# A sparse-expert block on one core: expert blocks of 32 rows in four column groups instead of 64 rows in two

## The chip, the cores and the metric

The program runs on one NeuronCore of one Trainium2 chip. The metric is the device time of one execution in microseconds (us); of the kernel before, three executions are given. Engines are named as the profile names them: PE (TensorE, with PEld for its weight loads), DVE (VectorE), ACT (ScalarE), POOL (GpSimd) and SP (SyncE).

## The reference

528 rows (16 learned ones and 512 tokens) of 1024 numbers go through one layer: a combined attention part, and then a layer of 32 experts of which each token takes its best four. Only the second part is touched:

```python
logits = xf @ w_router + b_router
top_val, top_idx = lax.top_k(logits, 4)
gates = softmax(top_val)
# for each token and each of its four experts e:
act = clamped_swiglu(x @ w1[e] + b1[e])      # w1[e]: 1024 x 2048
out[token] += gate * (act @ w2[e] + b2[e])   # w2[e]: 1024 x 1024
```

`clamped_swiglu` splits the 2048 columns into a gate and a linear half, clips both at 7, and gives gate * sigmoid(1.702 * gate) * (linear + 1). Everything is float32. An expert's weights are 12.58 MB, those of all 32 are 403 MB.

## The kernel before, in words

Attention, router and tables take the first 510 us or so of the span and are left as they are. The layer of experts takes the rest. It works in **blocks**: a block is up to SLOTS = 64 of the 512 * 4 = 2048 (token, expert) pairs, all of one expert. An expert with n pairs has ceil(n / 64) blocks, at least one. A token's 1024 numbers are stored as two rows of 512 (`xfd`), and the result as well (`accd`), so a block is 128 partitions: 64 slots times 2 half rows.

For block g the engines do, each in its own program order:

- DVE (`slot_list`, `slot_rows`) finds which tokens are in the block, with one small product on PE (`slot_product`, L1278), and writes their row numbers to `gidx`.
- POOL (`gather`, L445 and L446) fetches the rows by an indirect DMA into the one buffer `xg`.
- PE (`turn_x`, L1272) transposes `xg`, and ACT (`xT_copy`, L637) copies it to `xT`.
- PE (`up`, L1299 and L1305) makes the hidden layer: 8 contraction tiles k, two parts (gate, linear), two halves n of 512 columns. The stationary operand is 64 slots wide, and the two halves n go to partitions 0 to 63 and 64 to 127 of a bank, that is to two column groups of the array. L1305 adds the bias.
- DVE (`hidden`, L988 to L993) with ACT (L642) makes the activation `gat[b]`; PE (L1334) transposes it, and ACT (L655) copies it to `actT`.
- PE (`down`, L1326, bias L1341) makes the output in bank 4.
- DVE (L1018) scales it by the gate into the one buffer `yb` and keeps the row numbers (L1020).
- POOL (L466 and L467) adds the rows into `accd` by an indirect DMA that reads, adds and writes. Two such adds must not be in flight together, since they can touch one row; so POOL waits for the end of each (L470, and L471 marks it).

PE's loop over g is: `up(g+1)`, transposes of `gat(g)`, `turn_x(g+2)`, `slot_product(g+3)`, `down(g)`. SP fetches the weights in the order in which experts are worked on, into two sets of buffers (even and odd places): `w1` of the expert two places on is issued when the last `up` of this one is done (L383), and `w2` when the last `down` is done (L388). The order alternates experts with more than 64 pairs and others, as long as there are any.

The rows of each expert follow from the inputs. Reckoned from the reference's own router, the counts of the 32 experts are 83, 55, 79, 78, 107, 53, 17, 35, 43, 52, 104, 68, 116, 36, 99, 145, 59, 16, 8, 24, 38, 47, 44, 71, 90, 127, 51, 43, 57, 87, 42 and 74. In blocks of 64 that is 47 blocks, which is what the trace has; in blocks of 32 it is 81.

Of the kernel before, what the change touches and what calls it, by code (L numbers as in the profile page):

```python
# [30 lines left out]
P = 128  # L31
# [9 lines left out]
SLOTS = 64  # L41
# [12 lines left out]
C_ID, C_SLOT, C_EXP, C_D, C_B = 0, 128, 256, 320, 321  # L54
NCA = 322

T_TRI, T_ONE, T_IE, T_IG, T_THR = 0, 128, 256, 288, 288 + NG
NCT = T_THR + 8
# [12 lines left out]
def shape_constants():  # L71
# [4 lines left out]
    a[:, C_SLOT:C_SLOT + P] = c % SLOTS  # L76
    a[:, C_EXP:C_EXP + SLOTS] = np.where(p < 3 * NE, p % NE, -1)
# [5 lines left out]
    ct[:, T_THR:T_THR + 7] = SLOTS * np.arange(1, 8)  # L83
    ct[:, T_THR + 7] = 1e9
    half = (np.arange(P) >= SLOTS) * 1.0
# [29 lines left out]
def build(nc, I, out):  # L115
    ctx = ExitStack()
    with ctx:
# [80 lines left out]
        xg = work[:, 0:512]  # L198
        xT = work[:, 512:1024].rearrange("p (j n) -> p j n", j=4)
        gat = [work[:, 1024:1536], work[:, 1536:2048]]  # L200
        actT = work[:, 2048:2560].rearrange("p (j n) -> p j n", j=4)
# [15 lines left out]
        nbt = work[0:NE, o:o + 12]  # L217
        i8u = work[:, o + 13:o + 21].bitcast(U32)
        o += 21
# [18 lines left out]
        yb = sb("yb", [P, 512])[:, :]  # L238
# [12 lines left out]
        sidc = sb("sidc", [P, 1], I32)  # L251
# [38 lines left out]
        gather_turn, rows_turn, idx_kept = sem("gather_turn"), sem("rows_turn"), sem("idx_kept")  # L290
# [114 lines left out]
        def _(pool):  # L405
# [4 lines left out]
            zero = Steps(pool, zeros_ready)  # L410
            zero(nc.gpsimd.memset(qz[HD:P, :, 0, :], 0.0))
# [28 lines left out]
            def gather(n):  # L440

                if not (isinstance(n, int) and n == 0):
                    pool.wait_ge(gather_turn, n)
                pool.wait_ge(list_ready, n + 1)
                nc.gpsimd.tensor_tensor(sm[:, 36:37], ones1, ones1, ALU.mult).then_inc(gather_turn, 1)  # L445
                pool.indirect_dma_start(out=xg, out_offset=None, in_=xfd, in_offset=bass.IndirectOffsetOnAxis(  # L446
                    ap=gidx[:, 0:1], axis=0)).then_inc(xg_in, 16)
# [6 lines left out]
            nc.gpsimd.tensor_tensor(sm[:, 37:38], ones1, ones1, ALU.mult).then_inc(rows_turn, 1)  # L454
            nc.gpsimd.tensor_tensor(sm[:, 21:22], ones1, ones1, ALU.mult).then_inc(added, 1)
# [4 lines left out]
            with pool.Fori(0, MAXBLK) as g:  # L460
                with pool.If(g < nb):
                    pool.wait_ge(xT_done, g + 3)
                    gather(g + 3)
                    pool.wait_ge(rows_turn, g + 1)
                    pool.wait_ge(y_ready, 2 * g + 2)
                    nc.gpsimd.tensor_tensor(sm[:, 37:38], ones1, ones1, ALU.mult).then_inc(rows_turn, 1)  # L466
# [4 lines left out]
                    nc.gpsimd.tensor_tensor(sm[:, 21:22], ones1, ones1, ALU.mult).then_inc(added, 1)  # L471
                pool.nop()
# [5 lines left out]
        def _(act):  # L478
# [40 lines left out]
            for u, (g, f) in enumerate(units):  # L519
# [3 lines left out]
                if nq == 0:  # L523
                    act.wait_ge(zeros_ready, 2)
# [11 lines left out]
            def stick_log(hh):  # L536
                act.wait_ge(z_done, hh + 1)
                if hh == 0:
                    act.wait_ge(zeros_ready, 8)
# [51 lines left out]
            def diff_squares(i):  # L591
# [3 lines left out]
                act.activation(yb[:, 0:P], oall[:, i, :], ACT.Square,  # L595
# [39 lines left out]
            def xT_copy(n):  # L635
                act.wait_ge(xT_done, n + 1)
                act.activation(xT, PS[:, 7, :].rearrange("p (j n) -> p j n", j=4), ACT.Copy)\  # L637
                    .then_inc(xT_ready, 1)

            def sigmoid(n, b):  # L640
                act.wait_ge(gat_ready, n + 1)
                act.activation(PS[:, 2 * b, :], gat[b], ACT.Sigmoid, scale=HID_ALPHA).then_inc(sig_ready, 1)  # L642
# [28 lines left out]
        def _(dve):  # L671
# [237 lines left out]
            step(nc.vector.tensor_scalar(place[:, 0:1], nbt[:, 9:10], 1.0, None, ALU.is_gt))  # L909
# [3 lines left out]
            step(nc.vector.tensor_copy(nb2[:, 0:1], nbt[:, 9:10]))  # L913
# [18 lines left out]
            step(nc.vector.tensor_tensor(place[:, 8:9], place[:, 6:7], nbt[:, 9:10], ALU.subtract))  # L932
# [16 lines left out]
            def selector(n, b):  # L949

                nc.vector.tensor_scalar(selb[:, b, :], ca[:, C_EXP:C_EXP + SLOTS], egf[:, bass.ds(n, 1)], None,
                                        ALU.is_equal).then_inc(sel_ready, 1)

            def slot_list(n):
# [5 lines left out]
                for t in range(TT):  # L960
                    nc.vector.tensor_scalar(slots[:, t, :], ca[:, C_SLOT:C_SLOT + P], b64[:, bass.ds(n, 1)],  # L961
# [431 lines left out]
```

## Time and profile before

| what | value |
|---|---|
| three executions | 1656.5, 1657.3, 1658.1 us, median 1657.3 |
| the profiled execution: its span, first to last instruction | 1652.7 us |
| the same execution with what lies around the span | no time of its own is given; the median is 4.6 us above the span |
| PE busy | 1503.6 us, 91% of the span |
| POOL, ACT, DVE busy | 195.2, 266.2, 444.0 us |
| HBM read and written | 442.9 and 20.5 MB |
| TensorE clock, mean granted | 0.962 |
| products of `up` (L1299) and `down` (L1326), busy | 661.4 and 333.1 us |

A float32 product appears as two MATMUL records, so a block has 64 records of L1299 and 32 of L1326. Busy times of PE are unions: records of two column groups run at the same time, and the mean duration of one (597 ns) is longer than the time that each costs.

### The profile page before, as it was taken

To read this page: it belongs to the slowest core of one execution; us is meant where nothing else is said; L and a number is where in the kernel's file an instruction comes from. 1 tells how busy PE (TensorE), PEld (TensorE's weight loads), DVE (VectorE), ACT (ScalarE), POOL (GpSimd) and SP (SyncE) were. 2 spreads that over 40 slices of the span, in tenths; PEclk is the share of its full clock that TensorE was granted. 3 is DMA by queue.
4 is the path that set the end of the run, shared out by engine and by line. 5 is a ranking of instruction groups with operands and counts; after the bars stand their busy time and mean duration, and the time that the engine had idled before them with its cause. 6 is when DMAs were issued, how large, how long until landed. Compare 5 with 4: busy or idle time off the path is not lost.

```text
span 1652.7 us, 20407 instructions
## 1 busy us (share of the span) xinstructions
PE 1503.6 (91%) x6812; PEld 647.6 (39%) x6813; DVE 444.0 (27%) x1254; ACT 266.2 (16%) x444; POOL 195.2 (12%) x280
## 2 busy tenths in 40 slices
PE   5999988977965999999999999999999999999782
PEld 3746533355442343333334333333334334334231
DVE  3010123276253212222122221222212222122122
ACT  3001035343111101111011110111101111011012
POOL 5300000000000111111111111111111111111011
PEclk9999999987976999999999999999999999999997
DMA  9310020021645599999999999995999999999994
GB/s 322 98 38 0 0 102 0 0 106 64 254 156 226 224 349 374 413 374 406 374 374 413 374 406 373 374 370 223 388 375 405 380 394 388 368 406 383 406 403 140
DMA packets 95470, 463.71 MB, mean 281 GB/s; under 512 B 7316, under 2 KB 7572, under 8 KB 62676
## 3 DMA queue, kind: packets, MB, share of 16 engines
q1 hardware_dynamic: 84084, 436.90, 66.3%
q0 software_dynamic: 10976, 26.03, 6.3%
q10 hardware_dynamic: 384, 0.44, 0.1%
q8 instruction: 16, 0.26, 0.1%
q14 instruction: 10, 0.08, 0.0%
HBM read 442.86 MB, written 20.48 MB: 280 GB/s over the span
## 4 chain that ended last, share of the span: by engine, by line
PE 83%; DMA 5%; DVE 4%; issue 3%; ACT 2%; SPq 2%; POOL 0%; DVEq 0%; POOLq 0%; ACTq 0%
PE PS L1299 37%; PE PS L1326 18%; DMA sb_arena<-in_w 4%; PE PS L1067 3%; PE PS L1195 3%; PE PS L1073 3%; PE PS L1070 2%; PE PS L1071 2%; PE PS L1334 2%; PE PS L1272 1%; PE PS L1305 1%; PE PS L1091 1%; PE PS L1125 1%; PE PS L1104 1%; SPq L383 1%
## 5 line engine op out<-in xcount | busy, mean ns | idle before, releaser
L1299 PE MATMUL PS<-sb_arena,sb_work 128*64 128x512 f32 x3008 | 661.4, 597 | 17.8 <-DMA sb_arena<-in_w 16.1
L1299 PEld LDWEIGHTS PS<-sb_arena,sb_work 128*64 128x64 f32 x3008 | 230.7, 138 | 439.3 <-issue 414.7
L1326 PE MATMUL PS<-sb_arena,sb_work 128*64 128x512 f32 x1504 | 333.1, 595 | 13.0 <-issue 13.0
L988 DVE TENSOR_SCALAR sb_work<-PS 128x512 f32<-128x512 f32 x47 | 32.5, 692 | 638.3 <-PE PS L1305 638.3
L1326 PEld LDWEIGHTS PS<-sb_arena,sb_work 128*64 128x64 f32 x1504 | 112.9, 137 | 205.8 <-issue 205.4
L655 ACT ACTIVATE sb_work<-PS 128x512 f32<-128x512 f32 x47 | 28.1, 598 | 944.2 <-PE PS L1334 944.2
L467 POOL DMA_INDIRECT accd<-sb_yb,sb_sidc x47 | 75.4, 1605 | 7.2 <-issue 3.8
L1018 DVE TENSOR_SCALAR sb_yb<-PS,sb_gates 128x512 f32<-128x512 f32 x47 | 35.3, 751 | 131.5 <-PE PS L1326 131.5
L961 DVE TENSOR_SCALAR sb_slots<-sb_ca,sb_b,sb_rk 128x128 bf16<-128x128 f32 x204 | 56.9, 373 | 36.8 <-issue 36.8
L653 ACT ACT_TABLE_LOAD x47 | 60.3, 1283 | 0.8
L1195 PE MATMUL PS<-sb_arena 128*128 128x512 f32 x128 | 57.0, 604 | 1.5 <-DVE sb_arena L846 1.5
L445 POOL TENSOR_TENSOR sb_sm<-sb_sm 128x1 f32<-128x1 f32 x50 | 9.7, 193 | 410.8 <-DVE sb_gidx L979 410.3
L1067 PE MATMUL PS<-sb_arena 128*128 128x512 f32 x128 | 56.9, 606 | 0.6 <-DVE sb_work L713 0.6
L1073 PE MATMUL PS<-sb_arena 128*128 128x512 f32 x128 | 55.3, 592 | 0.0
L446 POOL DMA_INDIRECT sb_work<-xfd,sb_gidx x50 | 50.5, 1010 | 8.3 <-issue 2.2
L471 POOL TENSOR_TENSOR sb_sm<-sb_sm 128x1 f32<-128x1 f32 x47 | 8.9, 190 | 344.7 <-DMA accd<-sb_yb,sb_sidc 344.7
L1179 PE MATMUL PS<-sb_arena 128*128 128x128 f32 x112 | 22.8, 363 | 18.7 <-ACT sb_arena L587 17.4
L1070 PE MATMUL PS<-sb_arena 128*128 128x264 f32 x128 | 38.9, 386 | 0.0
L1071 PE MATMUL PS<-sb_arena 128*128 128x264 f32 x128 | 38.9, 386 | 0.0
L1067 PEld LDWEIGHTS PS<-sb_arena 128*128 128x128 f32 x128 | 24.8, 195 | 32.5 <-issue 31.3
L991 DVE TENSOR_TENSOR sb_work<-sb_work,PS 128x512 f32<-128x512 f32 x47 | 32.3, 688 | 18.9 <-ACT PS L642 18.9
L1195 PEld LDWEIGHTS PS<-sb_arena 128*128 128x128 f32 x128 | 24.6, 195 | 31.3 <-issue 29.5
(250 smaller groups left out, 1154.1 us busy)
## 6 DMA issues: line engine op xcount, KB each, us to landing
sb_arena<-in_w SPq DMA_DIRECT2D x192, 2048.0 KB, 20.6
sb_arena<-in_w_in SPq DMA_DIRECT2D x6, 2048.0 KB, 21.8
sb_arena<-in_x SPq DMA_DIRECT2D x8, 512.0 KB, 7.0
sb_arena<-in_w_out SPq DMA_DIRECT2D x2, 2048.0 KB, 10.7
accd<-sb_arena SPq DMA_DIRECT2D x4, 512.0 KB, 6.6
xfd<-sb_arena SPq DMA_DIRECT2D x4, 512.0 KB, 4.7
sb_arena<-accd SPq DMA_DIRECT2D x4, 512.0 KB, 6.6
out<-sb_arena SPq DMA_DIRECT2D x4, 512.0 KB, 2.8
```

The source lines that it names most:

```text
L446: pool.indirect_dma_start(out=xg, out_offset=None, in_=xfd, in_offset=bass.IndirectOffsetOnAxis(ap=gidx[:, 0:1], axis=0)).then_inc(xg_in, 16)
L467: pool.indirect_dma_start(out=acc, out_offset=bass.IndirectOffsetOnAxis(ap=sidc[:, 0:1], axis=0), in_=yb, in_offset=None, compute_op=ALU.a ...
L653: act.preload_act_table(ACT.Sigmoid)
L961: nc.vector.tensor_scalar(slots[:, t, :], ca[:, C_SLOT:C_SLOT + P], b64[:, bass.ds(n, 1)], rk[:, t, bass.ds(e, 1)], ALU.add, ALU.is_equal)\
L1018: nc.vector.tensor_scalar(yb, PS[:, 4, :], gates[:, bass.ds(g, 1)], None, ALU.mult)\
L1067: last = mm(PS[:, b, :], w[:, k, f * P:(f + 1) * P], nT[:, k, META:NKEY], **io)
L1070: mm(PS[:, b, 0:n], w[:, k, f * P:(f + 1) * P], nT[:, k, 0:n], **io)
L1071: last = mm(PS[:, b + 1, 0:n], w[:, k, f * P:(f + 1) * P], nT[:, k, n:NKEY], **io)
L1073: last = mm(PS[:, b, :], nT[:, k, META + f * P:META + (f + 1) * P], w[:, k, :], **io)
L1195: last = mm(PS[:, u % 4, :], mixT[:, k, t * P:(t + 1) * P], wo[:, n, k, :], start=k == 0, stop=k == KT - 1)
L1299: mm(PS[half(n), 2 * b + part, :], xT[:, k % 4, half(k // 4)], w[:, k, c:c + 512], start=k == 0, stop=False)
L1326: last = mm(PS[half(n), 4, :], actT[:, k % 4, half(k // 4)], w[:, k, n * 512:(n + 1) * 512], start=False, stop=k == KT - 1)
```

## The change

SLOTS becomes 32. A block is now 32 slots times 2 half rows, that is R = 64 partitions.

- `up` writes four column groups of 32 partitions into one bank: gate columns in groups 0 and 1, linear columns in 2 and 3. The number of products in a block is the same, each with a stationary operand of 32 columns instead of 64.
- `down` is split over the contraction too: the halves s of the contraction and the halves n of the columns go to four column groups, and the two halves s are added by DVE (`outputs`, one instruction more).
- The transposes stay 128 by 128 (rows 64 to 127 are filler); the copies of ACT take half the columns.
- Gathers and row adds move 64 rows each instead of 128.
- `yb` and `sidc` are doubled, and POOL's loop is turned round: it issues the row add of block g+1 in the turn of g, after it has seen the end of that of g.
- Tables for 81 instead of 47 blocks are a little longer.

```diff
-SLOTS = 64
+SLOTS = 32
...
-        gat = [work[:, 1024:1536], work[:, 1536:2048]]
+        gatp = [work[:, 1024:1536], work[:, 1536:2048]]
+        gat = [x[0:R, :] for x in gatp]
...
+            def scatter(n, b):
+
+                pool.wait_ge(added, n + 2)
+                pool.wait_ge(y_ready, 3 * n + 3)
+                nc.gpsimd.tensor_tensor(sm[:, 21:22], ones1, ones1, ALU.mult).then_inc(scatter_turn, 1)
+                pool.indirect_dma_start(out=acc, out_offset=bass.IndirectOffsetOnAxis(
+                    ap=sidc[0:R, b:b + 1], axis=0), in_=yb[b], in_offset=None,
+                    compute_op=ALU.add).then_inc(y_out, 16)
...
-            with pool.Fori(0, MAXBLK) as g:
-                with pool.If(g < nb):
-                    pool.wait_ge(xT_done, g + 3)
-                    gather(g + 3)
-                    pool.wait_ge(rows_turn, g + 1)
-                    pool.wait_ge(y_ready, 2 * g + 2)
-                    nc.gpsimd.tensor_tensor(sm[:, 37:38], ones1, ones1, ALU.mult).then_inc(rows_turn, 1)
-                    pool.indirect_dma_start(out=acc, out_offset=bass.IndirectOffsetOnAxis(ap=sidc[:, 0:1], axis=0),
-                                            in_=yb, in_offset=None, compute_op=ALU.add).then_inc(y_out, 16)
-                    pool.wait_ge(added, g + 1)
-                    pool.wait_ge(y_out, g * 16 + 16)
-                    nc.gpsimd.tensor_tensor(sm[:, 21:22], ones1, ones1, ALU.mult).then_inc(added, 1)
-                pool.nop()
+            scatter(0, 0)
+            with pool.Fori(0, (MAXBLK + 1) // 2) as i:
+                for b in range(2):
+                    g = 2 * i + b
+                    with pool.If(g < nb):
+                        pool.wait_ge(xT_done, g + 3)
+                        gather(g + 3)
+                        pool.wait_ge(scatter_turn, g + 1)
+                        pool.wait_ge(y_out, g * 16 + 16)
+                        nc.gpsimd.tensor_tensor(sm[:, 37:38], ones1, ones1, ALU.mult).then_inc(added, 1)
+                        with pool.If(g + 1 < nb):
+                            scatter(g + 1, 1 - b)
+                        pool.nop()
+                    pool.nop()
...
-                        dve.wait_ge(y_done, g + 1)
-                        dve.wait_ge(added, g + 1)
-                        nc.vector.tensor_scalar(yb, PS[:, 4, :], gates[:, bass.ds(g, 1)], None, ALU.mult)\
-                            .then_inc(y_ready, 1)
-                        nc.vector.tensor_copy(sidc[:, :], sidx[:, bass.ds(g, 1)]).then_inc(y_ready, 1)
+            def outputs(n, b):
+
+                gate = gates[0:R, bass.ds(n, 1)]
+                dve.wait_ge(y_done, n + 1)
+                dve.wait_ge(added, n + 1)
+                nc.vector.tensor_scalar(yb[b], PS[0:R, 4, :], gate, None, ALU.mult).then_inc(y_ready, 1)
+                nc.vector.tensor_copy(sidc[:, b:b + 1], sidx[:, bass.ds(n, 1)]).then_inc(y_ready, 1)
+                dve.wait_ge(y_ready, 3 * n + 2)
+                nc.vector.scalar_tensor_tensor(yb[b], PS[R:P, 4, :], gate, yb[b], ALU.mult, ALU.add)\
+                    .then_inc(y_ready, 1)
...
-                    for part in range(2):
-                        for n in range(2):
-                            c = part * D + n * 512
-                            mm(PS[half(n), 2 * b + part, :], xT[:, k % 4, half(k // 4)], w[:, k, c:c + 512],
-                               start=k == 0, stop=False)
+                    for c in range(4):
+                        mm(PS[group(c), b, :], xT[:, k % 4, group(k // 4)], w[:, k, c * 512:(c + 1) * 512],
+                           start=k == 0, stop=False)
...
-                for k in range(KT):
-                    if k % 4 == 0:
-                        pe.wait_ge(w2_full[par][k // 4], (at_place // 2) * 16 + 16)
-                    for n in range(2):
-                        last = mm(PS[half(n), 4, :], actT[:, k % 4, half(k // 4)], w[:, k, n * 512:(n + 1) * 512],
-                                  start=False, stop=k == KT - 1)
+                for j in range(4):
+                    for s in range(2):
+                        k = 4 * s + j
+                        if j == 0:
+                            pe.wait_ge(w2_full[par][s], (at_place // 2) * 16 + 16)
+                        for n in range(2):
+                            last = mm(PS[group(2 * s + n), 4, :], actT[:, j, group(s)],
+                                      w[:, k, n * 512:(n + 1) * 512], start=s == 1 and j == 0, stop=j == 3)
```

POOL's loop shows the new order. Before, one turn of the loop, for block g (`xfd` is read by the gather, `accd` is written by the row add; names in brackets are semaphores):

```order
L444 REGISTER_ALU [waits gather_turn,xT_done]
L445 TENSOR_TENSOR sb_sm<-sb_sm 128x1 [waits list_ready]
L446 DMA sb_work<-xfd,sb_gidx 128x512
L464 REGISTER_ALU
L465 ISA [waits rows_turn]
L466 TENSOR_TENSOR sb_sm<-sb_sm 128x1 [waits y_ready]
L467 DMA accd<-sb_yb,sb_sidc 1152x512
L470 ISA [waits added]
L471 TENSOR_TENSOR sb_sm<-sb_sm 128x1 [waits y_out]
```

With the change, one turn of the loop, on POOL as well (line numbers are those of the changed kernel here and below):

```order
L451 REGISTER_ALU [waits gather_turn,xT_done]
L452 TENSOR_TENSOR sb_sm<-sb_sm 128x1 [waits list_ready]
L453 DMA sb_work<-xfd,sb_gidx 64x512
L483 REGISTER_ALU
L484 ISA [waits scatter_turn]
L485 TENSOR_TENSOR sb_sm<-sb_sm 128x1 [waits y_out]
L486 COMPARE_AND_BRANCH
L466 ISA [waits added]
L467 TENSOR_TENSOR sb_sm<-sb_sm 128x1 [waits y_ready]
L468 DMA accd<-sb_work,sb_sidc 1152x512
```

In the turn of g the row add is that of g before, behind the gather of g+3; now it is that of g+1, so that the gather of g+3 stands behind the row add of g.

The other place is what DVE does with a block's output. Before:

```order
L1018 ISA [waits added,y_done]
L1018 TENSOR_SCALAR sb_yb<-PS,sb_gates 128x512
L1020 REGISTER_ALU
L1020 COPY sb_sidc<-sb_sidx 128x1
L951 ISA
L951 TENSOR_SCALAR sb_selb<-sb_ca,sb_egf 128x64
```

With the change, on DVE:

```order
L1019 ISA [waits added,y_done]
L1019 TENSOR_SCALAR sb_work<-PS,sb_gates 64x512
L1020 REGISTER_ALU
L1020 COPY sb_sidc<-sb_sidx 128x1
L1021 ISA
L1022 SCALAR_TENSOR_TENSOR sb_work<-PS,sb_gates,sb_work 64x512 [waits y_ready]
L968 ISA
L968 TENSOR_SCALAR sb_selb<-sb_ca,sb_egf 128x32
```

One instruction of 512 columns is added (L1022), which waits for the one ahead of it, and POOL's row add waits for it.

## Rows read from the trace of the kernel before

**Rows 1.** The page: busy time by engine, and the costliest group of instructions.

```profile
PE 1503.6 (91%) x6812; PEld 647.6 (39%) x6813; DVE 444.0 (27%) x1254; ACT 266.2 (16%) x444; POOL 195.2 (12%) x280
...
L1299 PE MATMUL PS<-sb_arena,sb_work 128*64 128x512 f32 x3008 | 661.4, 597 | 17.8 <-DMA sb_arena<-in_w 16.1
```

**Rows 2.** Busy time by stage, 1160 to 1500 us; columns in its first line.

```profile
core 0: us, PE busy (x) PEld busy (x) DVE busy (x) ACT busy (x) POOL busy (x), PEclk, DMA share, GB/s
...
1160.00:1500.00 340.00, 335.68 (x1691) 130.31 (x1688) 85.76 (x252) 43.28 (x60) 46.06 (x73) 1.00 0.99 391
```

**Rows 3.** Timeline of PE: start us, us, engine, line, operation, count, [idle before].

```profile
550.03 0.61 PE L1305 MATMUL PS<-sb_ball,sb_selb 128*64 128x512 bf16 x4
550.57 0.66 PE L1334 MATMUL PS<-sb_ca,sb_work 128*128 128x128 f32 x4
551.07 0.60 PE L1272 MATMUL PS<-sb_ca,sb_work 128*128 128x128 f32 x4
...
552.29 7.09 PE L1326 MATMUL PS<-sb_arena,sb_work 128*64 128x512 f32 x32 [0.21 <-issue]
559.20 13.91 PE L1299 MATMUL PS<-sb_arena,sb_work 128*64 128x512 f32 x64
...
573.47 0.66 PE L1334 MATMUL PS<-sb_ca,sb_work 128*128 128x128 f32 x4
```

**Rows 4.** Timeline of DVE after the down products of one block.

```profile
559.53 0.75 DVE L1018 TENSOR_SCALAR sb_yb<-PS,sb_gates 128x512 f32<-128x512 f32 x1 [2.67 <-PE PS L1326]
560.20 0.14 DVE L1020 COPY sb_sidc<-sb_sidx 128x1 int32 x1
```

**Rows 5.** Timeline of POOL: gathers (L446), row adds (L467), ends of adds (L471).

```profile
560.43 0.19 POOL L466 TENSOR_TENSOR sb_sm<-sb_sm 128x1 f32<-128x1 f32 x1 [4.29 <-DVE sb_sidc L1020]
560.77 1.63 POOL L467 DMA_INDIRECT accd<-sb_yb,sb_sidc  x1 [0.15 <-issue]
...
583.66 1.60 POOL L467 DMA_INDIRECT accd<-sb_yb,sb_sidc  x1
592.31 0.19 POOL L471 TENSOR_TENSOR sb_sm<-sb_sm 128x1 f32<-128x1 f32 x1 [7.05 <-DMA accd<-sb_yb,sb_sidc]
...
692.88 1.01 POOL L446 DMA_INDIRECT sb_work<-xfd,sb_gidx  x1
...
1111.69 1.60 POOL L467 DMA_INDIRECT accd<-sb_yb,sb_sidc  x1 [0.15 <-issue]
1116.46 0.20 POOL L471 TENSOR_TENSOR sb_sm<-sb_sm 128x1 f32<-128x1 f32 x1 [3.17 <-DMA accd<-sb_yb,sb_sidc]
...
1621.38 0.19 POOL L445 TENSOR_TENSOR sb_sm<-sb_sm 128x1 f32<-128x1 f32 x1 [0.47 <-issue]
1622.13 1.00 POOL L446 DMA_INDIRECT sb_work<-xfd,sb_gidx  x1 [0.57 <-issue]
```

**Rows 6.** Timeline, the first gather and the transposes that waited for it.

```profile
508.49 1.05 POOL L446 DMA_INDIRECT sb_work<-xfd,sb_gidx  x1 [0.15 <-issue]
...
511.98 1.12 PE L1272 MATMUL PS<-sb_ca,sb_work 128*128 128x128 f32 x4 [4.99 <-DMA sb_work<-xfd,sb_gidx]
```

**Rows 7.** DMA queues, 692.8 to 697.1 us: packets, MB, share of 16 engines.

```profile
q1 hardware_dynamic: 435, 1.81, 105.2%
```

**Rows 8.** DMA queues, 697.1 to 699.7 us.

```profile
q1 hardware_dynamic: 101, 0.80, 75.5%
q0 software_dynamic: 80, 0.26, 25.6%
```

**Rows 9.** Timeline of PE near the end, where it waits for weights.

```profile
1553.27 5.18 PE L1299 MATMUL PS<-sb_arena,sb_work 128*64 128x512 f32 x16 [3.07 <-DMA sb_arena<-in_w]
1558.95 3.65 PE L1299 MATMUL PS<-sb_arena,sb_work 128*64 128x512 f32 x16 [0.50 <-DMA sb_arena<-in_w]
...
1585.23 3.65 PE L1299 MATMUL PS<-sb_arena,sb_work 128*64 128x512 f32 x16 [2.77 <-DMA sb_arena<-in_w]
```

**Rows 10.** Busy time of the stretch behind the wait of 3.07 us.

```profile
1553.00:1556.40 3.40, 3.13 (x8) 1.00 (x10) 0.00 (x0) 0.00 (x0) 0.20 (x1) 0.50 1.01 420
```

More of the change, by code:

```diff
@@ L75, in shape_constants @@
     a[:, C_ID:C_ID + P] = p == c
-    a[:, C_SLOT:C_SLOT + P] = c % SLOTS
-    a[:, C_EXP:C_EXP + SLOTS] = np.where(p < 3 * NE, p % NE, -1)
+    a[:, C_SLOT:C_SLOT + SLOTS] = np.arange(SLOTS)
+    a[:, C_EXP:C_EXP + 1] = np.where(p < 3 * NE, p % NE, -1)
     ct = np.zeros((P, NCT), np.float32)
@@ L82, in shape_constants @@
     ct[:, T_IG:T_IG + NG] = np.arange(NG)
-    ct[:, T_THR:T_THR + 7] = SLOTS * np.arange(1, 8)
-    ct[:, T_THR + 7] = 1e9
-    half = (np.arange(P) >= SLOTS) * 1.0
+    ct[:, T_THR:T_THR + THR - 1] = SLOTS * np.arange(1, THR)
+    ct[:, T_THR + THR - 1] = 1e9
+    half = (np.arange(P) // SLOTS) % 2 * 1.0
     spare = 2 * T + np.arange(P)
@@ L197, in build @@
         work = sb("work", [P, 5 * 512])
[L198 to L201 removed]
+        R = 2 * SLOTS
+        xgp = work[:, 0:512]
+        xg = xgp[0:R, :]
+        xT = work[:, 512:768].rearrange("p (j n) -> p j n", j=4)
+        actT = work[:, 768:1024].rearrange("p (j n) -> p j n", j=4)
+        gatp = [work[:, 1024:1536], work[:, 1536:2048]]
+        gat = [x[0:R, :] for x in gatp]
         ct = work[:, 0:NCT]
@@ L216, in build @@
         o += NG // 2
-        nbt = work[0:NE, o:o + 12]
-        i8u = work[:, o + 13:o + 21].bitcast(U32)
-        o += 21
+        nbt = work[0:NE, o:o + 20]
+        nblk = nbt[:, 1 + THR:2 + THR]
+        i8u = work[:, o + 20:o + 28].bitcast(U32)
+        o += 28
         hot = work[0:NE, o:o + NREL]
@@ L237, in build @@
         g6 = sb("g6", [P, TT, NE, 6], BF16)
-        yb = sb("yb", [P, 512])[:, :]
+        yrow = sb("yb", [P, 512])[:, :]
+        yb = [yrow[0:R, :], work[0:R, 2048:2560]]
         rk = sb("rk", [P, TT, NE])
@@ L410, in _ @@
             zero = Steps(pool, zeros_ready)
+            zero(nc.gpsimd.memset(work[R:P, 1024:2048], 0.0))
             zero(nc.gpsimd.memset(qz[HD:P, :, 0, :], 0.0))
@@ L594, in diff_squares @@
                     act.wait_ge(osq_done, i)
-                act.activation(yb[:, 0:P], oall[:, i, :], ACT.Square,
+                act.activation(yrow[:, 0:P], oall[:, i, :], ACT.Square,
                                accum_out=ssd[:, i:i + 1]).then_inc(osq_done, 1)
@@ L636, in xT_copy @@
                 act.wait_ge(xT_done, n + 1)
-                act.activation(xT, PS[:, 7, :].rearrange("p (j n) -> p j n", j=4), ACT.Copy)\
+                act.activation(xT, PS[:, 7, :].rearrange("p (j n) -> p j n", j=4)[:, :, 0:R], ACT.Copy)\
                     .then_inc(xT_ready, 1)
@@ L1285, in expert, with group @@
                                      min_val=0, max_val=NE - 1)
-            def half(n):
+            def group(n):
                 return slice(n * SLOTS, (n + 1) * SLOTS)
@@ L1295, in up @@
                         pe.wait_ge(w1_full[par][k // 2], (at_place // 2) * 16 + 16)
-                    for part in range(2):
-                        for n in range(2):
-                            c = part * D + n * 512
-                            mm(PS[half(n), 2 * b + part, :], xT[:, k % 4, half(k // 4)], w[:, k, c:c + 512],
-                               start=k == 0, stop=False)
-                pe.wait_ge(sel_ready, g + 1)
-                for part in range(2):
-                    for n in range(2):
-                        c = part * D + n * 512
-                        last = mm(PS[half(n), 2 * b + part, :], selb[:, b, :], ball[:, c:c + 512],
-                                  start=False, stop=True)
+                    for c in range(4):
+                        mm(PS[group(c), b, :], xT[:, k % 4, group(k // 4)], w[:, k, c * 512:(c + 1) * 512],
+                           start=k == 0, stop=False)
+                pe.wait_ge(sel_ready, g + 1)
+                for c in range(4):
+                    last = mm(PS[group(c), b, :], selb[:, b, :], ball[:, c * 512:(c + 1) * 512],
+                              start=False, stop=True)
                 last.then_inc(up_done, 1)
@@ L1340, in finish_block @@
                 for n in range(2):
-                    mm(PS[half(n), 4, :], selb[:, b, :], ball[:, 2 * D + n * 512:2 * D + (n + 1) * 512],
+                    mm(PS[group(n), 4, :], selb[:, b, :], ball[:, 2 * D + n * 512:2 * D + (n + 1) * 512],
                        start=True, stop=False)
```

58 lines of the change are left out of this document (30 added, 28 removed).

## The prediction

> **What bounds the kernel now.** First I read the page's busy times: PE is busy for 91% of the span, and its largest group, the products of `up`, waits only 17.8 us in all, 16.1 of them for weights [rows 1]. So PE sets the pace. Second, the stages: in 340 us of the expert layer PE is busy for 335.7 at full clock, but the DMA engines are at 0.99 too, moving 391 GB/s [rows 2]. Two limits lie side by side, and taking work from PE alone can't gain much. Third, PE's timeline: from one block's transposes (550.57) to the next one's (573.47) are 22.90 us, of which `up` takes 13.91 and `down` 6.91 (552.29 to 559.20) [rows 3]. The 47 blocks and the waits make 47 * 22.90 + 17.8 = 1094 us.
>
> **PE's own work per block.** The 64 records of `up` cost 13.91 / 64 = 0.217 us each because two column groups run at once [rows 3]. With four at once a record costs half: `up` falls by 6.9 us, `down` by 3.5, the bias products of L1305 (0.54 to the next row) by 0.2. The transposes and the small products stay. A block then costs PE 22.90 - 10.6 = 12.3 us, say 12.4. No row shows four groups at once. The bounds are this and no overlap beyond two, which leaves 22.9; I take the full overlap, because two groups now show no loss at all (a record of 512 columns lasts 0.6 us and a pair costs 0.43), and it is the nearer row. By PE alone the layer would be 81 * 12.4 = 1004 us.
>
> **What DMA allows.** 30 experts' weights (377.5 MB; the first two are fetched mostly ahead) and 81 gathers and adds of 0.13 MB each way are 399 MB. At 391 GB/s [rows 2] that is 1020 us, so even at best no more than some 75 us are to be had.
>
> **The new loop through POOL.** This is the term that decides. The gather of block g+3 stands on POOL behind the row add of g, which waits for DVE's outputs of g, which wait for `down(g)`. The gather is needed by `turn_x(g+3)`, which PE reaches after only one `up`. Before, that gather was issued ahead of the add of g and had all of `down(g)` and a 13.9 us `up` as cover; now its cover is an `up` of 7 us. One turn, from the start of one `turn_x` to that of the next:
>
> - `turn_x` to the first product of `down`: 552.29 - 551.07 = 1.2 us [rows 3];
> - `down`: half of 7.09, with its tail 3.6 [rows 3];
> - end of `down` (559.38) to POOL's L466 (560.43): 1.05 us [rows 3 to 5], and the added DVE instruction, taken as long as its neighbour's 0.75 [rows 4] with 0.1 for its wait: 1.9;
> - L466 to the issue of the add: 0.34 [rows 5];
> - the issue: 1.6 us for 128 rows [rows 5]; for 64 between 0.8 (all of it per row) and 1.6 (none); I take 1.3;
> - from the add's end to the gather's start on a POOL that is itself late: 0.47 + 0.75 = 1.2 (the two rows from 1621.38) [rows 5];
> - the gather's flight.
>
> Without the flight that is 9.8 us. The flight is 3.5 us when nothing else is in the queues (508.49 to 511.98, reader included) [rows 6]. While weights are streaming it is longer: a gather issued at 692.88 [rows 5] had moved nothing by 697.1, when only the weight queue had packets [rows 7], and its 80 packets fell in the next 2.6 us [rows 8], so it took between 4.2 and 6.8 us. The row adds agree: 8.65 us to the row behind them with weights in flight, 4.77 without [rows 5]. With half the rows I take 2.9 and 6.1. The turn is then 12.7 us in a quiet queue and 15.9 behind weights, against 12.4 of PE's work: PE waits up to 3.5 us in a block. Bounds: 9.3 + 5.2 = 14.5 to 10.1 + 6.8 = 16.9 behind weights, 12.4 to 13.6 without.
>
> The Trainium skill (DMA: Bandwidth & Descriptors, Queues, rings and completion order) says that each DMA engine goes round its queues packet by packet, by which a gather would hardly feel the weights; rows 7 and 8 contradict that for this kernel, and the measurement decides. What follows if it held for smaller gathers is the first rival.
>
> **The clock.** Near the end PE waits 3.07 us, and the next 16 records take 5.18 us instead of 3.65 [rows 9], since the clock was granted at 0.50 for that stretch, that is 1.2 instead of 2.4 GHz [rows 10]; after a wait of 2.77 us they take 3.65 [rows 9]. A wait of 3.5 us per block lies above both, so this may cost 0 to 1.5 us in each such block. I take 0.5: a slow stretch that falls on `up` is covered by the same wait.
>
> **Other terms.** Row adds stay in order; the add of g+1 waits for the end of that of g, some 7 us after the start of a turn plus 8.7 [rows 5], which is before the next is due at 7 + 16, so double buffering neither costs nor gives. It only hides a wait of POOL for which PE was not waiting. ACT's copies and DVE's steps of a block (under 9 us of busy time) are covered by a turn of 12 or more; longer tables and one more memset at the start cost a microsecond at most, beside loads. Waits for weights shrink, since the stage becomes slower than DMA: the 17.8 us go.
>
> **The sum.** Weights stream for 377.5 MB / 391 GB/s = 965 us, three quarters of a stage of 1250, so 60 blocks of 81 turn in 15.9 + 0.5 = 16.4 us and 21 in 12.7: 984 + 267 = 1251 us, against 1094. That is +157: the profiled span of 1652.7 becomes 1810, and the median of 1657.3, which is 4.6 above it, **1814**. With the low bounds 60 * 14.5 + 21 * 12.4 = 1130, +36; with the high ones and the whole clock term 60 * 18.4 + 21 * 13.6 = 1390, +296. Most of this case lies in 1715 to 1900.
>
> **Rival 1, the gather is quick enough; faster or level.** If a gather of 64 rows waits for about one weight packet per packet of its own, its flight stays near 3 us and the turn near 12.6. Then weights set the pace where experts are small: 5 of the 15 later pairs of experts have only 4 blocks, 50 us of PE against 25.2 MB / 391 GB/s = 64 us of DMA. 81 * 12.6 + 5 * 14 = 1091, and with 12.4 a block 1074: 1637 to 1655, **1645**. For it: fewer packets. Against it: the delay in rows 7 and 8 lies ahead of the first packet, and fewer rows don't shorten that. The point at which it decides is a flight of about 3 us behind weights. The skill's round-robin rule above speaks for this rival. Chance 0.21.
>
> **Rival 2, four groups overlap only in part.** If a record costs 0.135 us and not 0.108, PE's block is 15 us and the turn 0.9 longer, so 60 * 17.3 + 21 * 15 = 1353, +259: **1916**. The Trainium skill (TensorE: Matmul & The Clock Gate, Measured speedup vs the span model) has 2.38 times from three column tiles, which is such a loss of a fifth; no row here shows one for two. Chance 0.08.
>
> **Rival 3, the change doesn't do what it says:** the groups run two at a time as now, and 81 blocks cost 22.9 each: 1855, +761, **2418**. Chance 0.04.
>
> **How the numbers follow.** My forecast has 0.67. A difference of less than 0.2% (3.3 us) can't be told from no change here. Rival 1 gives 0.16 of faster and 0.04 of same, the rest of it is just slower; my case and rivals 2 and 3 are slower, 0.80 in all. The range holds my case but for its upper end and rival 1 but for its lowest part: 1640 to 1900. My case's own is 1715 to 1900.
>
> **What the profile after would show.** Right: 81 blocks; L1323 at about 6.9 us a block; most of PE's idle time in front of L1298, released by the gather's DMA, some 3 us each; a PE clock below 1.00 in many slices; DMA below 0.85 in the layer. Wrong: PE's waits in front of L1323 and L1350, released by weights, with DMA at 0.99 (rival 1); `up` at 8.6 us (rival 2) or 13.9 (rival 3).

## The result, and the profile after

The changed kernel takes 2009.59 us (median of 4 runs, 2008.37 to 2016.81) beside 1656.88 us for the kernel before (4 runs, 1653.69 to 1658.1): a ratio of 1.2146, 95% interval 1.2117 to 1.2175. It is slower, as forecast, but by 353 us and not by 157, and lies outside the range. The profiled execution has a span of 2007.3 us, 354.6 more than before.

The page of the changed kernel, busy time and the granted clock by slice, then the groups that answer to [rows 1], and the gather:

```profile
PE 1608.3 (80%) x10688; PEld 630.4 (31%) x10689; DVE 709.9 (35%) x1913; ACT 342.4 (17%) x580; POOL 288.8 (14%) x450
...
PEclk9999899897788887989888888898888888888886
...
L1323 PE MATMUL PS<-sb_arena,sb_work 128*32 128x512 f32 x5184 | 573.9, 594 | 2.2 <-ACT sb_work L654 2.2
...
L1298 PE MATMUL PS<-sb_ca,sb_work 128*128 128x128 f32 x332 | 60.4, 310 | 218.2 <-DMA sb_work<-xfd,sb_gidx 218.2
...
L453 POOL DMA_INDIRECT sb_work<-xfd,sb_gidx x84 | 79.6, 948 | 13.8 <-issue 13.8
```

5184 records of L1323 are 81 blocks of 64. `up` no longer waits for weights at all; nearly all idle time of PE that another engine or a transfer causes (213.7 of 215.9 us) has moved in front of L1298, the transposes of the gathered rows. The granted clock stands at 7 or 8 tenths in nearly every slice of the layer.

PE's waits of the changed kernel, 520 to 1990 us (line, what it waited for, us in total, times, longest; "issue" is idle time for which the profile shows no releaser):

```profile
PE PS L1298 <- DMA sb_work<-xfd,sb_gidx: 213.7, 60, 6.4
PE PS L1365 <- issue: 47.9, 81, 0.6
PE PS L1304 <- issue: 15.4, 49, 0.4
```

Busy time by stage of the changed kernel, to lay beside [rows 2]: us, busy time and count of PE, PEld, DVE, ACT, POOL, then clock, DMA share, GB/s. PE and DMA, both full before, are both partly idle now.

```profile
600.00:1000.00 400.00, 324.36 (x2568) 108.69 (x2564) 147.02 (x400) 57.71 (x88) 69.02 (x114) 0.88 0.76 284
...
1500.00:1900.00 400.00, 318.97 (x2464) 104.65 (x2466) 142.49 (x388) 55.22 (x84) 64.47 (x108) 0.86 0.80 304
```

One turn of the loop behind weights, in three timelines of the changed kernel (start us, us, engine, line, operation, what it writes and reads, count, [idle before and its releaser]). PE, the place of [rows 3]:

```profile
860.61 0.66 PE L1298 MATMUL PS<-sb_ca,sb_work 128*128 128x128 f32 x4 [3.13 <-DMA sb_work<-xfd,sb_gidx]
861.57 0.59 PE L1304 MATMUL PS<-sb_g,sb_slots 128*128 x4 [0.31 <-issue]
862.74 0.61 PE L1365 MATMUL PS<-sb_ball,sb_selb 128*32 128x512 bf16 x2 [0.58 <-issue]
863.42 5.92 PE L1350 MATMUL PS<-sb_arena,sb_work 128*32 128x512 f32 x32
869.14 7.06 PE L1323 MATMUL PS<-sb_arena,sb_work 128*32 128x512 f32 x64
876.01 0.41 PE L1327 MATMUL PS<-sb_ball,sb_selb 128*32 128x512 bf16 x4
...
880.47 0.66 PE L1298 MATMUL PS<-sb_ca,sb_work 128*128 128x128 f32 x4 [3.46 <-DMA sb_work<-xfd,sb_gidx]
```

DVE, the place of [rows 4]:

```profile
869.52 0.74 DVE L1019 TENSOR_SCALAR sb_yb<-PS,sb_gates 64x512 f32<-64x512 f32 x1 [4.18 <-PE PS L1350]
...
870.36 0.75 DVE L1022 SCALAR_TENSOR_TENSOR sb_yb<-PS,sb_gates,sb_yb 64x512 f32<-64x512 f32 x1
```

POOL, the place of [rows 5]:

```profile
871.19 0.20 POOL L467 TENSOR_TENSOR sb_sm<-sb_sm 128x1 f32<-128x1 f32 x1 [11.85 <-DVE sb_yb L1022]
871.53 1.44 POOL L468 DMA_INDIRECT accd<-sb_yb,sb_sidc  x1
872.51 0.70 POOL L452 TENSOR_TENSOR sb_sm<-sb_sm 128x1 f32<-128x1 f32 x1
873.36 0.95 POOL L453 DMA_INDIRECT sb_work<-xfd,sb_gidx  x1 [0.16 <-issue]
```

Read the three together and the ring of the prediction is there, link by link: the transposes at 860.61, `down` from 863.42 to 869.34, DVE to 871.11, POOL's add at 871.53, the gather at 873.36, the next transposes at 880.47 after 3.46 us of idle PE. Of this turn of 19.86 us, 7.11 are the gather. And `up` is what was hoped of four groups: 64 records in 7.06 us against 13.91 before [rows 3].

Why `down` takes 5.92 us here is in the stages of the changed kernel (same columns as above): behind the wait the clock is granted at 0.50, 1.2 instead of 2.4 GHz, and the low stretch covers `down`, not `up`.

```profile
847.60:861.20 13.60, 10.47 (x98) 3.29 (x88) 4.45 (x8) 0.98 (x2) 3.00 (x5) 1.00 0.76 268
861.20:868.00 6.80, 5.84 (x31) 2.08 (x34) 2.22 (x10) 1.67 (x2) 0.00 (x0) 0.50 1.03 423
```

That holds for the whole trace. Of 79 turns (all but the first), 57 begin behind a wait of over 1 us, and `down` takes 4.70 to 6.36 us in every one of them; of the other 22 it takes 3.64 us in 21.

From the same 79 turns I took five pieces, start of the transposes to start of the next. 58 turns end in a wait of over 1 us (the loaded turns; beside them the forecast for turns behind weights), 21 don't (the quiet turns; beside them the one for quiet queues):

| piece of a turn, us | forecast, behind weights | measured, 58 turns | forecast, quiet | measured, 21 turns |
|---|---|---|---|---|
| `turn_x` to first product of `down` | 1.2 | 2.56 | 1.2 | 2.42 |
| `down` | 3.6 | 5.31 | 3.6 | 4.78 |
| end of `down` to L467 | 1.9 | 1.88 | 1.9 | 1.89 |
| L467 to start of the gather | 2.84 | 2.18 | 2.84 | 2.17 |
| start of the gather to the next `turn_x` | 6.1 | 7.16 | 2.9 | 3.48 |
| clock, as a term of its own | 0.5 | in the above | 0 | in the above |
| turn | 16.4 | 19.09 | 12.7 | 14.74 |

The mean of all turns is 17.93 us; 81 of them are 1452 us, against the 1094 of the layer before: +358, within 4 us of the difference of the spans. So the lost time is all in these turns.

The quiet turns need a second look. PE's rows where one of them ends (the next `turn_x` is L1298 at 825.23):

```profile
824.74 0.66 PE L1358 MATMUL PS<-sb_ca,sb_work 128*128 128x128 f32 x4
825.23 0.60 PE L1298 MATMUL PS<-sb_ca,sb_work 128*128 128x128 f32 x4
```

L1298 follows L1358 with no idle time, as in 20 of the 21 quiet turns. So what closes a quiet turn is PE's own work, and the 3.48 us of its last piece are not a gather's flight.

### The profile page after: what moved, and what is told of

Same layout as the page of the kernel before. It is cut to its first block, busy times and chain, and to the rows that moved or that the text cites. A ratio compares the mean times of both kernels' runs of the same rounds, so it can differ in the third digit from the quotient of the medians.

```text
span 2007.3 us, 31695 instructions
## 1 busy us (share of the span) xinstructions
PE 1608.3 (80%) x10688; PEld 630.4 (31%) x10689; DVE 709.9 (35%) x1913; ACT 342.4 (17%) x580; POOL 288.8 (14%) x450
## 4 chain that ended last, share of the span: by engine, by line
issue 59%; PE 22%; POOL 8%; DVE 4%; DMA 3%; ACT 2%; POOLq 1%; SPq 0%; DVEq 0%; ACTq 0%
POOL sb_work L453 4%; PE PS L1093 3%; PE PS L1221 3%; PE PS L1099 3%; POOL sb_sm L452 3%; DMA sb_work<-xfd,sb_gidx 2%; PE PS L1350 2%; PE PS L1096 1%; PE PS L1097 1%; POOL accd L468 1%; PE PS L1117 1%; PE PS L1151 1%; PE PS L1205 1%; PE PS L1323 1%; POOL sb_sm L485 1%
## 5 line engine op out<-in xcount | busy, mean ns | idle before, releaser
L1323 PE MATMUL PS<-sb_arena,sb_work 128*32 128x512 f32 x5184 | 573.9, 594 | 2.2 <-ACT sb_work L654 2.2
L1350 PE MATMUL PS<-sb_arena,sb_work 128*32 128x512 f32 x2592 | 418.2, 804 | 2.4 <-issue 1.0
L1323 PEld LDWEIGHTS PS<-sb_arena,sb_work 128*32 128x32 f32 x5184 | 168.4, 110 | 393.0 <-issue 392.7
L1298 PE MATMUL PS<-sb_ca,sb_work 128*128 128x128 f32 x332 | 60.4, 310 | 218.2 <-DMA sb_work<-xfd,sb_gidx 218.2
L1007 DVE TENSOR_SCALAR PS<-PS 64x512 f32<-64x512 f32 x81 | 56.8, 701 | 423.5 <-PE PS L1327 423.5
L672 ACT ACTIVATE sb_work<-PS 128x256 f32<-128x256 f32 x81 | 31.1, 384 | 1015.0 <-PE PS L1358 1015.0
L1350 PEld LDWEIGHTS PS<-sb_arena,sb_work 128*32 128x32 f32 x2592 | 103.0, 142 | 272.3 <-issue 271.5
L467 POOL TENSOR_TENSOR sb_sm<-sb_sm 128x1 f32<-128x1 f32 x81 | 15.7, 194 | 882.1 <-DVE sb_yb L1022 452.5
L1298 PEld LDWEIGHTS PS<-sb_ca,sb_work 128*128 128x128 f32 x332 | 39.9, 153 | 233.3 <-DMA sb_work<-xfd,sb_gidx 232.5
L1365 PE MATMUL PS<-sb_ball,sb_selb 128*32 128x512 bf16 x162 | 44.5, 543 | 47.9 <-issue 47.9
L1010 DVE TENSOR_TENSOR sb_work<-sb_work,PS 64x512 f32<-64x512 f32 x81 | 55.0, 679 | 53.5 <-ACT PS L659 53.5
L1304 PE MATMUL PS<-sb_g,sb_slots 128*128 x336 | 47.6, 180 | 24.2 <-issue 15.4
L654 ACT ACTIVATE sb_work<-PS 128x256 f32<-128x256 f32 x83 | 31.3, 377 | 195.9 <-PE PS L1298 195.9
L452 POOL TENSOR_TENSOR sb_sm<-sb_sm 128x1 f32<-128x1 f32 x84 | 57.5, 684 | 23.9 <-DVE sb_gidx L998 23.9
L485 POOL TENSOR_TENSOR sb_sm<-sb_sm 128x1 f32<-128x1 f32 x81 | 15.7, 194 | 299.4 <-DMA accd<-sb_yb,sb_sidc 152.1
```

The costliest lines, as they stand in the source:

```text
L1298: last = nc.tensor.transpose(PS[:, 7, j * P:(j + 1) * P], xgp[:, j * P:(j + 1) * P], ident)
L1323: mm(PS[group(c), b, :], xT[:, k % 4, group(k // 4)], w[:, k, c * 512:(c + 1) * 512], start=k == 0, stop=False)
L1350: last = mm(PS[group(2 * s + n), 4, :], actT[:, j, group(s)], w[:, k, n * 512:(n + 1) * 512], start=s == 1 and j == 0, stop=j == 3)
```

## The experiments

The theory at this point: the add ahead of the gather puts the gather's flight into PE's path; the waits it causes bring the low clock, which lengthens `down`, which stands in the same ring. The rivals: PE's smaller blocks or the double-buffered adds cost the time, and the low clock is only a sign of waits; or the order on POOL alone is at fault, whatever the size of a block. A run with one measurement carries no interval; two runs of one kernel differ here by up to 0.8% (1634.41 to 1647.45 for the first below), so nothing under some 13 us is read from it. Experiments 1, 3, 4 and 6 ran on one chip (the kernel before: 1656.92 us), 2, 5 and 7 on another (1652.25).

### 1. The gather ahead of the add again

The one edit that undoes the order on POOL and keeps the rest:

```diff
+            pool.wait_ge(xT_done, 3)
+            gather(3)
             scatter(0, 0)
...
-                    with pool.If(g < nb):
-                        pool.wait_ge(xT_done, g + 3)
-                        gather(g + 3)
+                    with pool.If(g + 1 < nb):
+                        pool.wait_ge(xT_done, g + 4)
+                        gather(g + 4)
...
-                        with pool.If(g + 1 < nb):
-                            scatter(g + 1, 1 - b)
-                        pool.nop()
+                        scatter(g + 1, 1 - b)
```

> Theory (the gather of block g+3 waits on POOL behind the row add of g, and PE waits for it and then runs at the low clock): with the gather issued first, PE's 214 us of waits in front of L1298 go, the granted clock is 1.00 again, and a turn costs 12.4 to 13 us; 81 turns with some 70 us of waits for weights are 1075 to 1120 us against about 1435 now, so 1650 to 1695 us. Rival (81 blocks simply have too many fixed steps, wherever the gather stands): within 2% of 2009 us.

Measured: 1642.09 us (6 runs, 1634.41 to 1647.45), ratio to the kernel before 0.9918, interval 0.9887 to 0.9948. It is 367 us faster than the changed kernel and 0.8% faster than the kernel before; that lies 8 us below the range expected, whose 70 us of waits for weights were too many. Its PE waits, 520 to 1990 us:

```profile
PE PS L1323 <- DMA sb_arena<-in_w: 52.1, 20, 6.4
PE PS L1365 <- issue: 8.8, 20, 0.7
...
PE PS L1298 <- DMA sb_work<-xfd,sb_gidx: 2.0, 1, 2.0
```

Its POOL timeline in one turn, the transposes that the gather is for, and its stage from 600 to 1000 us:

```profile
834.91 1.44 POOL L468 DMA_INDIRECT accd<-sb_yb,sb_sidc  x1
...
843.46 0.95 POOL L453 DMA_INDIRECT sb_work<-xfd,sb_gidx  x1
```

```profile
851.93 0.60 PE L1298 MATMUL PS<-sb_ca,sb_work 128*128 128x128 f32 x4
```

```profile
600.00:1000.00 400.00, 386.62 (x3582) 141.21 (x3578) 202.24 (x562) 79.51 (x124) 95.84 (x157) 0.99 1.01 388
```

The gather starts as soon as its indices are there and has 8.5 us until the transposes at 851.93 need it. The median turn is 12.35 us, the 12.4 worked out for PE alone, the clock is back, and what PE waits for is weights at 388 GB/s. The order on POOL carries the whole loss.

### 2. The adds waited for in the same turn

Is it the double buffering of the adds? This kernel keeps both buffers and the gather first, but waits for each add before the next turn:

```diff
-            scatter(0, 0)
...
                         gather(g + 3)
+                        scatter(g, b)
                         pool.wait_ge(scatter_turn, g + 1)
...
-                        with pool.If(g + 1 < nb):
-                            scatter(g + 1, 1 - b)
-                        pool.nop()
```

> The kernel as changed with POOL's order of before: gather of g+3, row add of g, wait for that add, all in one turn (both buffers for the output rows stay). Theory (the place of the gather is all that matters, the overlapped adds give nothing): POOL is free again 1.9 + 1.8 + 7.3 = 11 us after the end of down, and the next gather can't start before its list, 12.6 us after it (843.12 against the down that ends at 831 in the gather-first run), so the same time as gather first, 1642 us within 8. Rival (the double buffer is what makes gather-first quick): the add's wait shows in the turns, 1 us or more in each, 1720 us or more.

Measured: 1645.95 us (4 runs, 1640.85 to 1651.0), ratio 0.9948, interval 0.9928 to 0.9968; the median turn is 12.37 us. Its waits, all engines, 520 to 1620 us:

```profile
POOL sb_sm L485 <- DMA accd<-sb_work,sb_sidc: 221.2, 40, 6.4
POOL sb_sm L485 <- DMA accd<-sb_yb,sb_sidc: 214.8, 40, 6.3
```

POOL stands 436 us in waits for adds, and PE waits for none of them. The intervals of this kernel and of experiment 1 overlap, so the overlapped adds are worth nothing that these runs can tell. This settles a point which the diff hides: the order on POOL came with the double buffering, and the time is lost by that order, not gained by the buffers.

### 3. The same order in the kernel before

Blocks of 64, two groups, one buffer, as before; only POOL's loop is in the changed order (the add of g+1 at the end of turn g, ahead of the next gather).

```diff
+            pool.wait_ge(rows_turn, 1)
+            scatter(0)
...
-                    pool.wait_ge(rows_turn, g + 1)
-                    pool.wait_ge(y_ready, 2 * g + 2)
...
+                    with pool.If(g + 1 < nb):
+                        scatter(g + 1)
```

> The kernel before (blocks of 64) with the changed kernel's order on POOL: the gather of g+3 behind the row add of g. Theory (the order is harmful only because the cover is now one short up): the loop is 1.2 + 7.1 + 1.05 + 0.34 + 1.6 + 0.4 + 7.0 = 18.7 us, less than a block's 22.9, so no change, 1657 us within 5. Rival (the order of POOL costs by itself, whatever the block's size): at least 3 us more in each of 47 blocks, 1800 us.

Measured: 1664.0 us in one run, beside 1656.92 (9 runs). Its PE waits, 520 to 1990 us:

```profile
PE PS L1306 <- DMA sb_arena<-in_w: 13.6, 7, 3.2
...
PE PS L1279 <- DMA sb_work<-xfd,sb_gidx: 6.9, 1, 6.9
```

One wait for a gather, the first, and the median turn is 22.90 us in both kernels. The order costs nothing that can be told where `up` lasts 13.9 us: the gather, 9.5 us in flight here, is still covered. By the sum of the expectation with 9.5 for its 7.0 the ring is 21.2 us, so it was covered with 1.7 us to spare, not 4.2. So neither the order alone nor the small block alone loses the time (that of experiment 1 has small blocks and is fast); it takes both. The 7.1 us above the kernel before, 2 more than expected at most, are within what one run can't tell.

### 4. The changed kernel with thin weights

To take the weights' traffic away and leave everything else: of each expert but the first two, only 128 of the 2048 columns of w1 and 64 of the 1024 of w2 are fetched; the products run on what lies there. The fetch of the other weights is what this kernel leaves out.

```diff
-                        sp.dma_start(w1t(par)[:, 2 * c:2 * c + 2, :],
-                                     I["w1"][bass.ds(e, 1), 2 * c * P:2 * (c + 1) * P, :]
+                        sp.dma_start(w1t(par)[:, 2 * c:2 * c + 2, 0:128],
+                                     I["w1"][bass.ds(e, 1), 2 * c * P:2 * (c + 1) * P, 0:128]
```

> The kernel as changed, but from the third expert on only one in sixteen columns of its weights is fetched, so that DMA queues are nearly empty (the outputs are then wrong). Theory: every gather lands in 2.5 to 3.4 us, every turn is a quiet one of about 13.3 us, PE waits under 1 us a block and the clock stays up: 81 * 13.3 = 1077 us against 1435, about 1650 us. Rival (the gathers' flight does not depend on the weights): 2009 us within 2%.

Measured: 1647.04 us. Of its PE waits, 520 to 1990 us:

```profile
PE PS L1365 <- issue: 48.7, 81, 0.6
PE PS L1298 <- DMA sb_work<-xfd,sb_gidx: 7.6, 5, 6.5
```

The clock is 1.00 and the mean turn 13.40 us (nine in ten lie between 13.1 and 13.9): 2.21 to `down`, 3.66, 1.94, 2.17, and 3.42 from the gather on. PE waits for a gather in 5 turns only, though the ring's flight of 2.9 us is there in each: this turn is PE's own work. The flight is what changed, as the issues of the trace show, 520 to 1600 us (issues, median us from issue to landing). The changed kernel:

```profile
sb_work<-xfd,sb_gidx POOLq DMA_INDIRECT x61, 7.0
accd<-sb_yb,sb_sidc POOLq DMA_INDIRECT x30, 7.3
```

With thin weights:

```profile
sb_work<-xfd,sb_gidx POOLq DMA_INDIRECT x80, 2.9
accd<-sb_yb,sb_sidc POOLq DMA_INDIRECT x40, 3.7
```

Gather ahead of the add, full weights (experiment 1):

```profile
sb_work<-xfd,sb_gidx POOLq DMA_INDIRECT x81, 6.3
```

Blocks of 64, gather behind an add of 128 rows (experiment 3):

```profile
sb_work<-xfd,sb_gidx POOLq DMA_INDIRECT x46, 9.5
```

Four flights of the gather, three with 64 rows and the last with 128: 2.9 us with hardly any weights in the queues, 6.3 behind weights with no add ahead, 7.0 right behind an add of 64 rows, 9.5 right behind one of 128. The weights' traffic costs a gather of 64 rows some 4 us (7.0 against 2.9, both right behind an add), and the add ahead of it in the same software queue a further 0.7. With 128 rows the gather behind an add takes at least 2.7 us more than the one without, which took 4.2 to 6.8 [rows 7, 8].

### 5. Gather first and thin weights together

Both edits of experiments 1 and 4; it leaves out the same part of the weights.

> Gather first, and from the third expert on one in sixteen columns of the weights is fetched (wrong outputs). Theory (gather first is bound by the weights, not by PE): turns of 12.35 us throughout, 81 * 12.35 = 1000 against about 1075 to 1100, so 1545 to 1565 us. Rival (PE or the small steps bind gather first as well): 1640 us.

Measured: 1550.19 us; the median turn is 12.15 us at a clock of 1.00. Of its PE waits, 520 to 1990 us:

```profile
PE PS L1298 <- DMA sb_work<-xfd,sb_gidx: 2.0, 1, 2.0
PE PS L1365 <- issue: 1.2, 2, 0.6
```

The kernel of experiment 1 is therefore bound by weights: they cost it some 90 us (one run, and on another chip), 52.1 in PE's waits for them, an estimated 26 in the low clock behind such waits (51 us of the layer at 0.50, none here) and 16 in the turns, 0.2 us longer each (12.35 and 12.15). That is the prediction's first paragraph: taking work from PE can't gain much with DMA at 0.99. And L1365 has its gap of 0.6 us in 81 turns of experiment 4 and in 2 of this one, and the turn is 13.40 us there and 12.15 here. The two kernels differ in POOL's order alone.

### 6. Idle products in the wait

Does the low clock cost time in the ring? Here PE does 14 products whose result nobody reads just ahead of the transposes, some 3.2 us more work in each block:

```diff
                 last.then_inc(actT_done, 1)
+                for _ in range(14):
+                    mm(PS[R:P, 3, :], ball[:, 0:R], ball[:, 0:512], start=True, stop=True)
                 turn_x(g + 2)
```

> The kernel as changed, with 14 idle products of 512 columns (3.0 us at full clock) put into the place where PE waits for the gather; they touch no result. If the low clock behind the wait is what lengthens the turns from about 16 to 19.5 us, the clock stays near 1.00, the turns behind weights fall to about 16.4 us and the quiet ones rise from 13.3 to 16.3: 81 * 16.4 = 1330 instead of 1435, about 1900 us, faster by added work. If the clock costs nothing on this path, the long turns stay at 19.5 and only the quiet ones grow: 2060 us or more.

Measured: 1961.41 us, 48 us less than the changed kernel with 260 us more of PE's work:

```profile
L1361 PE MATMUL PS<-sb_ball 128*64 128x512 bf16 x1134 | 259.9, 381 | 0.0
```

Its stages from 600 to 1900 us are at a clock of 0.97, 0.99 and 0.97, and PE's timeline shows what a turn behind weights is with the clock kept:

```profile
837.24 0.66 PE L1298 MATMUL PS<-sb_ca,sb_work 128*128 128x128 f32 x4 [0.65 <-DMA sb_work<-xfd,sb_gidx]
838.21 0.55 PE L1304 MATMUL PS<-sb_g,sb_slots 128*128 x4 [0.31 <-issue]
...
839.78 3.64 PE L1350 MATMUL PS<-sb_arena,sb_work 128*32 128x512 f32 x32
...
854.63 0.66 PE L1298 MATMUL PS<-sb_ca,sb_work 128*128 128x128 f32 x4 [0.41 <-DMA sb_work<-xfd,sb_gidx]
```

17.39 us (the median of all turns is 17.36), with `down` at 3.64: the ring without the clock's share. The changed kernel's 19.09 less 2.0 us of clock, worked out below, would be 17.1, so most of the clock's share is seen by itself. The mean over all turns is only 0.7 us lower, 17.26 against 17.93: in the quiet turns the added 3.2 us of work lie open, and 18 of 80 turns still have a slow `down` (5.05 to 5.34 us, as at 857.31), behind waits of only 0.2 to 1.3 us. The theory has the direction and the rival, 2060 us or more, is out by this one run, but the gain is less than half of the one I had expected; the gaps in front of L1304 and of `down` stay, too.

### 7. Half of the idle products

Seven products instead of 14, otherwise the same edit.

> As the run with 14 idle products, with 7 of them (1.5 us). Theory (a wait of about 2 us leaves the clock up more often than one of 3.5): long turns 17 to 18, quiet ones 14.8, 1900 to 1950 us, below the run with 14. Rival (any wait of 2 us brings the low clock as before): long turns 19.5, quiet 14.8, about 2040 us.

Measured: 2005.1 us, level with the changed kernel. Its PE timeline:

```profile
850.86 1.70 PE L1361 MATMUL PS<-sb_ball 128*64 128x512 bf16 x7
854.64 0.66 PE L1298 MATMUL PS<-sb_ca,sb_work 128*128 128x128 f32 x4 [2.09 <-DMA sb_work<-xfd,sb_gidx]
...
857.31 6.25 PE L1350 MATMUL PS<-sb_arena,sb_work 128*32 128x512 f32 x32
```

PE now waits 2.1 us in place of 3.5, and `down` is as slow as ever. From 540 to 1920 us the clock is low for 280 us, against 352 in the changed kernel and 61 in experiment 6. My expectation of a part of the gain failed; the time is between theory and rival and nearer to the rival: behind most of these waits of 2 us the clock is still low.

## Why the prediction was right in sign and wrong in size

**What bounds, right.** Two limits side by side: with the gather out of the way the layer is held by weights at 388 GB/s (experiment 1), and by PE at 12.15 us a block without them (experiment 5).

**PE's own work, right.** L1323 takes 7.06 us for 64 records, 6.9 to the next row, as forecast. Rivals 2 and 3 (groups overlapping in part, or two at a time) are out. The 2.38 that the Trainium skill has for three column tiles (TensorE: Matmul & The Clock Gate, Measured speedup vs the span model) would be a loss of a fifth; no run here has one tile or three, but from two groups to four none is seen in these f32 products (13.91 to 7.06 us).

**The ring through POOL, right as a mechanism.** 81 blocks, the waits in front of L1298, 60 of them, 213.7 us or 3.6 each, and DMA at 0.73 to 0.80 are what the prediction named as the signs of its case. Undoing the order takes all of it away (experiment 1), and the same order costs nothing that can be told in the larger blocks (experiment 3).

**Rival 1, wrong.** It needed a flight of about 3 us behind weights; 64 rows take 6.3 with nothing of their own queue ahead, against 6.1 forecast. With 128 rows one gather took 4.2 to 6.8 [rows 7, 8], so half the rows don't shorten it to what the rival needed. The Trainium skill (DMA: Bandwidth & Descriptors, Queues, rings and completion order) says that engines go round the queues packet by packet. What was drawn from it, that a gather would hardly feel the weights, is contradicted again, 2.9 us without them and 6.3 with them; in which order an engine takes packets no run here shows. 1645 us is reached only with the gather moved.

**The sum, too small by 204 us.** 60 turns of 19.09 and 21 of 14.74 are 1455 us; I had 1251. The count of turns behind weights, 60, was met (58 to 60), in part by luck: it was three quarters of a stage of 1250 us, and for the 1455 measured the same working gives 54. The steps that failed, each by its term:

- *"A slow stretch that falls on `up` is covered by the same wait … I take 0.5."* It falls on `down`, which stands inside the ring: 5.31 instead of 3.66 us, and 0.35 more ahead of it, 2.0 us a loaded turn. Quiet turns pay 1.3: 13 of the 21 begin behind the wait that ended the turn before and have a `down` of 5.47 us on average, the other 8 have 3.64. 60 * 2.0 + 21 * 1.3 = 147 us, less the 30 forecast: +117. The bound of 1.5 was itself too low.
- *"`turn_x` to the first product of `down`: 1.2."* Taken from a turn in which PE didn't wait, and given no bound. At full clock it is 2.2 (experiment 4): 81 us. The gaps in the rows are 0.3 in front of L1304 and 0.6 in front of L1365, marked "issue". The one in front of L1365 is there where the gather only just arrives, even where no wait of the engine is seen (all 81 turns of experiment 4), and rarer where it is early (20 turns of experiment 1, 2 of experiment 5). My reading is that PE's sequencer is held at the wait and can't work ahead through the register loads and branches behind it; that was argued from the rows, not tried by itself.
- *"With half the rows I take 2.9 and 6.1."* From the gather's start to the transposes it is 7.16 and 3.48: 60 * 1.06 + 21 * 0.58 = 76 us. Behind weights, 64 of them, the 6.1 holds for a gather by itself (6.3 in experiment 1); what I left out is the add issued 1.8 us earlier in the same queue, and the 5.2 of my low bound had no row behind it. In quiet turns the flight was right, 2.9 (experiment 4). The other 12 us belong to PE: its own work is not 12.4 us in such a turn but 12.15 (experiment 5) plus the gaps, some 13.2, and ends after the gather has landed.
- *The issue of the add, 1.3, and 1.2 to the gather.* 2.18 instead of 2.84, since the gather's preparation L452 starts before the add's row ends (872.51 and 872.97): 81 * 0.66 = 53 us less.
- A slip of addition: the links without the flight come to 9.54, and I wrote 9.8. That is 21 us in the other direction.

117 + 81 + 76 - 53 - 21 = 200 of the 204. The high bounds, 18.4 and 13.6 us a turn, were passed by 0.7 and 1.1, and by the two terms that had no upper bound or too small a one. **Both lie in the same place, PE's restart after a wait.** I priced the wait and not what comes behind it.

## What to carry to other kernels

A transfer that the next block needs within a few microseconds must not stand in program order behind a store that waits for this block's result; nobody needs that store soon. Halving a block halves the cover of everything that has a fixed time in flight, so look for each such transfer at how long it is covered before and after, not at how much work is saved; here an order that cost nothing to speak of under 13.9 us of `up` cost 22% under 7. And a short wait of TensorE in each turn of a ring is to be priced with its tail: the products behind it at half the clock and the gaps before its sequencer is ahead again, here 2.0 and 1.0 us on a wait of 3.6.

## What was not expected of the hardware

- Issuing an indirect transfer costs POOL almost the same for half the rows: 1.44 us for an add of 64 rows and 1.60 for 128 [rows 5], 0.95 and 1.01 for a gather. The flight of a gather with no add ahead is 6.3 us behind weights with 64 rows (experiment 1), and lay between 4.2 and 6.8 in one case with 128 [rows 7, 8].
- The granted clock was 0.50 from 840.8 to 847.6, again from 861.2 to 868.0, and so on in every turn that begins behind a wait of over 1 us, here waits of 3.1 to 3.6. In experiment 7 it was low after waits of 2.0 to 2.7 us too, and in experiment 6 after 18 of 0.2 to 1.3 us, whereas before the change 16 records took their normal 3.65 us after one of 2.77 [rows 9]. So the length of the last wait alone does not decide it (PE also idles some 1.0 us more in each such turn, in front of L1304 and L1365); what else does stays open.
- 260 us of work that nobody needs made a kernel 48 us faster (experiment 6), since they kept the clock in most turns and lay in the wait; seven products instead of 14 gained nothing (experiment 7).
